# Seven block products for eight in the layers' down projection

## What is computed

```python
def conv_ffn(hn, w_up, conv_w, conv_b, w_down):
    u = depthwise_conv_centred(hn @ w_up, conv_w, conv_b)
    gate, val = jnp.split(u, 2, axis=-1)
    return (jax.nn.gelu(gate, approximate=True) * val) @ w_down

for l in range(DEPTH_2):                                   # 2 layers
    mixed = hybrid_mixer(rms_norm(x, mix_pre_g[l]), ...)
    x = x + rms_norm(mixed, mix_post_g[l])
    ff = conv_ffn(rms_norm(x, ffn_pre_g[l]), w_up[l], ...)
    x = x + rms_norm(ff, ffn_post_g[l])
```

## Time and profile before

| | us |
|---|---|
| median of 3 runs | 2075.01 (2074.34 to 2078.17) |
| the profiled execution | 2079.1 |
| its span, first to last instruction | 2077.4 |
| TensorE busy | 1974.8 (95%) |
| VectorE busy | 597.2 (29%) |
| ScalarE busy | 409.3 (20%) |
| GpSimd busy | 92.5 (4%) |

### The profile page before, as it was taken

How to read it: one execution, slowest core, us unless ns; L and a number is a source line. 1 busy time by engine, 2 the same in 40 slices (tenths; PEclk the granted TensorE clock), 3 DMA queues, 4 the chain that set the end, 5 groups by cost and what they waited for, 6 DMA issues and landing times.

```text
span 2077.4 us, 22981 instructions
## 1 busy us (share of the span) xinstructions
PE 1974.8 (95%) x9060; PEld 1137.3 (55%) x9060; DVE 597.2 (29%) x1240; ACT 409.3 (20%) x868; POOL 92.5 (4%) x167
## 2 busy tenths in 40 slices
PE   6999999999989899999898999999999999999998
PEld 2767885333333333333333334766888456778863
DVE  1387513122112112211121122542333035333311
ACT  2134213111111001111110112243222023422110
POOL 0000000000000000000000000200000011000000
PEclk9999999999999999999999999999999999999999
DMA  9655358999999999999999998153454334335430
GB/s 377 236 195 206 129 203 322 411 427 427 428 427 428 428 427 428 428 427 427 428 428 428 428 427 341 40 204 112 143 162 162 120 114 162 122 122 162 162 139 24
DMA packets 132852, 582.20 MB, mean 280 GB/s; under 512 B 9608, under 2 KB 55824, under 8 KB 106416
## 3 DMA queue, kind: packets, MB, share of 16 engines
q1 hardware_dynamic: 128240, 574.70, 69.5%
q0 software_dynamic: 4544, 6.57, 1.0%
HBM read 580.18 MB, written 2.63 MB: 281 GB/s over the span
## 4 chain that ended last, share of the span: by engine, by line
PE 74%; DMA 21%; DVE 3%; ACT 1%; issue 1%; SPq 0%; DVEq 0%; ACTq 0%
PE psum L357 52%; PE psum L675 11%; DMA work<-w_gu 11%; DMA ring<-w_gu 9%; PE psum L620 9%; PE psum L2118 1%; DVE work L1778 1%; PE psum L662 1%; DMA ring<-w_in 1%; PE psum L651 1%; DMA ring<-w_ada 0%; PE psum L1052 0%; ACT work L2439 0%; SPq L459 0%; DVE work L1776 0%
## 5 line engine op out<-in xcount | busy, mean ns | idle before, releaser
L357 PE MATMUL psum<-normed,ring 128*128 128x256 f32 (+1 forms) x2432 | 507.5, 370 | 0.2 <-PE psum L357 0.2
L357 PEld LDWEIGHTS psum<-normed,ring 128*128 128x128 f32 x2432 | 443.0, 191 | 60.8 <-issue 4.7
L620 PE MATMUL psum<-ring,normed 128*64 128x512 f32 x1024 | 234.5, 611 | 35.0 <-DMA ring<-w_gu 33.8
L620 PE MATMUL psum<-work,normed 128*64 128x512 f32 x1024 | 232.6, 608 | 33.1 <-DMA work<-w_gu 33.1
L357 PE MATMUL psum<-ring,work 128*128 128x512 f32 (+1 forms) x592 | 249.8, 581 | 0.1
L357 PE MATMUL psum<-work 128*128 128x128 f32 (+7 forms) x1152 | 185.1, 334 | 2.5 <-ACT work L2429 1.7
L357 PEld LDWEIGHTS psum<-ring,work 128*128 128x128 f32 x592 | 111.7, 190 | 130.6 <-issue 129.3
L620 PEld LDWEIGHTS psum<-ring,normed 128*64 128x64 f32 x1024 | 81.0, 141 | 186.3 <-issue 184.1
L620 PEld LDWEIGHTS psum<-work,normed 128*64 128x64 f32 x1024 | 80.5, 140 | 183.6 <-issue 183.6
L357 PEld LDWEIGHTS psum<-work 128*128 128x128 f32 (+2 forms) x1152 | 135.1, 186 | 65.0 <-issue 52.0
L357 PE MATMUL psum<-ring,normed 128*128 128x512 f32 (+2 forms) x400 | 160.5, 557 | 2.2 <-DMA ring<-w_in 1.8
(11 more groups left out here) (304 smaller groups left out, 1326.7 us busy)
## 6 DMA issues: line engine op xcount, KB each, us to landing
ring<-w_gu SPq DMA_DIRECT2D x64, 2048.0 KB, 27.4
work<-w_gu SPq DMA_DIRECT2D x64, 2048.0 KB, 27.5
work<-w_dn SPq DMA_DIRECT2D x32, 2048.0 KB, 27.4
ring<-w_dn SPq DMA_DIRECT2D x28, 2048.0 KB, 27.4
ring<-w_in SPq DMA_DIRECT2D x25, 2048.0 KB, 9.2
ring<-w_up SPq DMA_DIRECT2D x44, 1024.0 KB, 7.3
ring<-w_ada SPq DMA_DIRECT2D x11, 2048.0 KB, 9.4
ring<-w_down SPq DMA_DIRECT2D x10, 2048.0 KB, 7.8
```

The lines of the kernel that those rows point to most:

```text
L357: return pe.matmul(out, lhsT, rhs, start=first, stop=last, **kw)
L620: ins = pe.matmul(b[r], self.hgT[:, 2 * q + k, r], ws[e][:, k, n0:n0 + 512], start=q == 0 and k == 0, stop=q == QUARTERS - 1 and k == 1, s ...
```

## The change

Chunks 0 to 15 are taken as 8 pairs (SEVENS = 8), a pair a, b = 2i, 2i + 1. For a pair, the 2x2 blocks are A[t][k] = the tokens t of chunk k, and B[k][j] = half j of the weights of chunk k. Their product, four output blocks with two products each, is formed from seven products (Winograd's form of Strassen's algorithm) of these operands:

- tokens: A11, A12, A22 as they are, and four sums S1 = A21 + A22, S2 = S1 - A11, S3 = A11 - A21, S4 = A12 - S2. GpSimd makes them for four pairs at a time, 128x512 per operation, when eight chunks of `hid` are ready. They lie in SBUF where the attention's inputs were.
- weights: B11, B21 as they are, T1 = B12 - B11, T3 = B22 - B12 (written over B12 in the ring slot), T2 = B22 - T1, T4 = B21 - T2. VectorE makes them pair by pair, four operations of 128x512. T1, T2, T4 go into one of two buffers; the sums for pair i wait for TensorE to be through with pair i - 2 (`weight_sums_used`).

The seven products of all eight pairs add up in seven PSUM banks; three of these are directly output blocks (`down` (0,0), (0,1), (1,0)), four are named `sum`. After the eighth pair ScalarE copies `sum` 1 and VectorE combines the `sum` banks into four totals in SBUF (`sevens_totals`). Chunks 16 to 21 are done as before, four products each, on top of the three output banks and, for (1,1), in a bank of its own. VectorE then adds each finished bank to its total, and `post_norm` goes on from the total in SBUF.

The core of the diff:

```diff
-    u += [("down", l, t, j) for t in tiles for j in range(2)]
+    u += [("sum", l, 1), ("down", l, 0, 0), ("down", l, 0, 1), ("sum", l, 7), ("down", l, 1, 0), ("sum", l, 5), ("sum", l, 6), ("down", l, 1, 1)]
...
+            for g in range(SEVENS // 4):
+                pool.wait_ge(hid_ready, l * FC + 8 * g + 8)
+                pairs = hid[:, 8 * g:8 * g + 8].rearrange("p (i k) t -> p i k t", k=2)
+                a11, a12, a21, a22 = (pairs[:, :, k, t * P:(t + 1) * P] for t in range(2) for k in range(2))
+                s1, s2, s3, s4 = (s_sums[:, i, 4 * g:4 * g + 4] for i in range(4))
+                step(pool.tensor_tensor(s1, a21, a22, ALU.add))
+                step(pool.tensor_tensor(s3, a11, a21, ALU.subtract))
+                step(pool.tensor_tensor(s2, s1, a11, ALU.subtract))
+                pool.tensor_tensor(s4, a12, s2, ALU.subtract).then_inc(s_ready, 1)
...
-            for d in range(4):
-                w = weights(d)
-                for k in range(4):
-                    if (d, k) == (0, 0):
-                        pe.wait_ge(hid_ready, l * FC + 16)
-                    for t in range(NT):
-                        for j in range(2):
-                            ins = product(t, j, 4 * d + k, w[:, k])
-                ins.then_inc(down_used, 1)
+            def seven(i, w):
+                a, b = 2 * i, 2 * i + 1
+                wa, wb = w[:, a % 4], w[:, b % 4]
...
+                total(1, product(("sum", l, 1), tokens(a, 0), half(wa, 0), True))
+                product(("down", l, 0, 0), tokens(b, 0), half(wb, 0))
+                product(("down", l, 0, 1), s_sums[:, 3, i], half(wb, 1))
+                pe.wait_ge(t_ready, l * SEVENS + i + 1)
+                total(7, product(("sum", l, 7), s_sums[:, 2, i], half(wa, 1), True))
+                ins = product(("down", l, 1, 0), tokens(b, 1), t_sums[:, i % 2, 2])
+                if i % 2 == 1:
+                    ins.then_inc(down_used, 1)
+                total(5, product(("sum", l, 5), s_sums[:, 0, i], t_sums[:, i % 2, 0], True))
+                ins = product(("sum", l, 6), s_sums[:, 1, i], t_sums[:, i % 2, 1], True)
+                if last:
+                    total(6, ins)
+                else:
+                    ins.then_inc(t_used, 1)
...
             for t in range(NT):
                 for j in range(2):
-                    if (t, j) == (1, 1) and l + 1 < LAYERS:
-                        norm_transposes(l + 1, 0, 0)
-                    for k in range(16, FC):
-                        ins = product(t, j, k, ws[k // 4 - 4][:, k % 4])
+                    if (t, j) == (1, 1):
+                        empty("down", l, 1, 1)
+                    for k in range(2 * SEVENS, FC):
+                        if (t, j, k) == (1, 1, FC - 3) and l + 1 < LAYERS:
+                            norm_transposes(l + 1, 0, 0)
+                        ins = matmul(pe, bank("down", l, t, j), tokens(k, t), half(ws[k // 4 - SEVENS // 2][:, k % 4], j),
+                                     (t, j, k) == (1, 1, 2 * SEVENS), k == FC - 1)
                     ins.then_inc(*B.fills("down", l, t, j))
...
+            take(totals[:, 1], bank("sum", l, 1), "sum", l, 1)        # ScalarE
...
+                if s == 1:
+                    total = totals[:, 1 + 2 * t + j]
+                    filled("down", l, t, j)
+                    take(TT(total, bank("down", l, t, j), total, ALU.add), "down", l, t, j)
+                    step(TT(half(xn[:, t], j), total, half(post[:, s], j), ALU.mult))
+                    continue
...
+            def weight_sums(i):
+                if i >= 2:
+                    dve.wait_ge(t_used, l * (SEVENS - 1) + i - 1)
+                if i % 2 == 0:
+                    dve.wait_ge(*S.ready("down", l, i // 2))
+                w = slot(S.no(("down", l, i // 2)), 4, D)
+                wa, wb = w[:, 2 * i % 4], w[:, 2 * i % 4 + 1]
+                t1, t2, t4 = (t_sums[:, i % 2, n] for n in range(3))
+                step(TT(t1, half(wa, 1), half(wa, 0), ALU.subtract))
+                step(TT(half(wa, 1), half(wb, 1), half(wa, 1), ALU.subtract))
+                step(TT(t2, half(wb, 1), t1, ALU.subtract))
+                TT(t4, half(wb, 0), t2, ALU.subtract).then_inc(t_ready, 1)
+
+            def sevens_totals():
+                both, s00, s01, s10, s11 = (totals[:, n] for n in range(5))
+                dve.wait_ge(*B.released("sum", l, 1))
+                filled("sum", l, 6)
+                take(TT(both, bank("sum", l, 6), s00, ALU.add), "sum", l, 6)
+                step(TT(s01, bank("sum", l, 5), both, ALU.add))
+                filled("sum", l, 7)
+                take(TT(s10, bank("sum", l, 7), both, ALU.add), "sum", l, 7)
+                take(TT(s11, bank("sum", l, 5), s10, ALU.add), "sum", l, 5)
+
             for c in range(FC):
                 outer_taps(c)
                 if c >= 1:
                     hidden(c - 1)
+                if c in (FC - 2, FC - 1):
+                    weight_sums(c - (FC - 2))
             hidden(FC - 1)
+            for i in range(2, SEVENS):
+                weight_sums(i)
+            sevens_totals()
             post_norm(l, 1, 0)
```

More of the change, by code:

```diff
@@ L2005, in second_block @@
     taps = Arena(mem.work, ex_at).take(3, 2, L)
+    s_sums = Arena(mem.work, aqk_at).take(4, SEVENS, P)
+    t_sums = Arena(mem.work, mqk_at).take(2, 3, 512)
+    totals = Arena(mem.work, mqk_at).take(5, 512)
+    assert aqk_at + 4 * SEVENS * P <= hid_at and SEVENS % 4 == 0 and SEVENS * 2 == FC - FC % 4 - 4
     assert hid_at + FC * L <= mqk_at
@@ L2324, in down @@
         def down(l):
-            for t in range(NT):
-                for j in range(2):
-                    empty("down", l, t, j)
-            def product(t, j, k, w):
-                return matmul(pe, bank("down", l, t, j), hid[:, k, t * P:(t + 1) * P], w[:, j * 512:(j + 1) * 512], k == 0, k == FC - 1)
             def weights(d):
@@ L2334, in weights, with tokens @@
                 return slot(S.no(("down", l, d)), min(4, FC - 4 * d), D)
[L2336 to L2344 removed]
+            def tokens(k, t):
+                return hid[:, k, t * P:(t + 1) * P]
@@ new lines, in seven, with product, total @@
+            def seven(i, w):
+                a, b = 2 * i, 2 * i + 1
+                wa, wb = w[:, a % 4], w[:, b % 4]
+                last = i == SEVENS - 1
+                def product(name, lhsT, rhs, ends=False):
+                    if i == 0:
+                        empty(*name)
+                    return matmul(pe, bank(*name), lhsT, rhs, i == 0, ends and last)
+                def total(n, ins):
+                    if last:
+                        ins.then_inc(*B.fills("sum", l, n))
+                total(1, product(("sum", l, 1), tokens(a, 0), half(wa, 0), True))
[8 more added lines that the diff above has]
+                ins = product(("sum", l, 6), s_sums[:, 1, i], t_sums[:, i % 2, 1], True)
+                if last:
+                    total(6, ins)
+                else:
+                    ins.then_inc(t_used, 1)
@@ L2345, in down @@
+            pe.wait_ge(hid_ready, l * FC + 2 * SEVENS)
+            for i in range(SEVENS):
+                if i % 4 == 0:
+                    pe.wait_ge(s_ready, l * (SEVENS // 4) + i // 4 + 1)
+                if i % 2 == 0:
+                    w = weights(i // 2)
+                seven(i, w)
             pe.wait_ge(hid_ready, (l + 1) * FC)
-            ws = [weights(d) for d in range(4, DOWN_SLOTS)]
+            ws = [weights(d) for d in range(SEVENS // 2, DOWN_SLOTS)]
             for t in range(NT):
@@ L2454, in pre_norm @@
                 else:
[L2455 to L2456 removed]
+                    act.wait_ge(*(B.released("mix", l, t, j) if s == 1 else (x_new, 4 * (l - 1) + 2 * t + j + 1)))
                 squares(half(x[:, t], j), ssq, n, j)
@@ L2467, in post_norm @@
             for j in range(2):
-                act.wait_ge(*B.ready(kinds[s], l, t, j))
-                squares(bank(kinds[s], l, t, j), psq, n, j, post_squared)
+                act.wait_ge(*(B.released("down", l, t, j) if s == 1 else B.ready("mix", l, t, j)))
+                squares(totals[:, 1 + 2 * t + j] if s == 1 else bank("mix", l, t, j), psq, n, j, post_squared)
             mean_root(psq, pr, n).then_inc(post_rstd, 1)
@@ L2645, in post_norm @@
             for j in range(2):
-                take(STT(out=half(x[:, t], j), in0=half(xn[:, t], j), scalar=pr[:, n, 1:2], in1=half(x[:, t], j), op0=ALU.mult, op1=ALU.add),
-                     kinds[s], l, t, j)
+                ins = STT(out=half(x[:, t], j), in0=half(xn[:, t], j), scalar=pr[:, n, 1:2], in1=half(x[:, t], j), op0=ALU.mult, op1=ALU.add)
+                if s == 1:
+                    signal(ins, x_new, 4 * l + 2 * t + j + 1)
+                else:
+                    take(ins, "mix", l, t, j)
         def conv(l, p):
```

22 lines of the change are left out of this document (12 added, 10 removed).

## The result

The changed kernel takes 2062.11 us (median of 4 runs, 2061.07 to 2063.57) where the kernel before took 2074.70 us beside it (4 runs, 2074.34 to 2078.17): a ratio of 0.9935, 95% interval 0.9921 to 0.9949. The forecast was 2060.8 us, with a range of 2058.0 to 2065.0. The profiled run of the changed kernel took 2061.15 us (span 2059.4 us), that of the kernel before 2079.1 us (span 2077.4).

The account below looks back on a forecast made before the run. It took the down projections to be paced by TensorE's number of products. Terms of -13.73, +0.2, -0.98 and +0.26 sum to -14.25 us, from 2075.0 to 2060.8 us; range 2058.0 to 2065.0.

Parts of the forecast that it names:

- Term 1: Down projections: 80 products for 88 per layer at 0.858 us each, saving 6.87 us a layer, 13.73 us in two.
- Term 2: Down projections: some 15 more waits per layer on TensorE's products, taken as 0.1 us a layer, 0.2 us in all.
- Term 3: End of layer 0: longer chain but three more products of cover; idle goes, transposes take 0.87 for 1.09 us; gain 0.98 us.
- Term 4: End of layer 1: the chain longer by an addition is not covered by products, costing 0.26 us.
- waits that are not free: Rival, 12%: each met wait breaks TensorE's stream by up to 0.1 us; gain shrinks by up to 3 us, 2062 to 2064.
- The sums in time: Down projections: VectorE's weight sums, 0.692 us each, cost TensorE nothing; narrowest place is pair 1 with 1.8 us to spare.
- the rival's working: Rival, 3%: VectorE sets the down projections' pace from 1.50 us per operation; at 9.3 us a pair, 2111 us.
- What I feared for `up`: In `up`, each of four GpSimd operations may hold up VectorE's `hidden` by up to 1.4 us, at zero cost.
- late next: After layer 0's end, the new x^T must be in `normed` before layer 1's first product; holds by 1.3 us.
- the narrower one: Run time if the forecast as worked out holds: 2059.5 to 2062.0 us, given 75%.

Follow-up runs that it names:

- eight_products: Changed kernel with each pair's first product computed twice, so eight products a pair, all waits and sums kept: 2075.16 us, ratio 0.9997.
- no_weight_sums2: Changed kernel without all weight sums, their waits and counts; products take plain weight halves, slots are counted free a little later: 2063.25 us, ratio 0.9940.
- transposes_alone: Kernel before the change, with only the transposes of the next layer's x moved three products later: 2078.18 us in a single run.
- token_sums_late: Changed kernel with GpSimd's second group of token sums waiting for all 22 chunks of `hid`, beside the weight sums: 2060.11 us in a single run.
- the second measurement: The changed kernel timed again with no edit: 2061.92 us against 2075.87 us, ratio 0.9934.

## Why the prediction was right

Its steps against the traces (us, negative is faster):

| step | forecast | measured | from |
|---|---|---|---|
| Term 1, 16 products | -13.73 | -13.74 | 7.85 - 0.98 and 6.87; eight_products -6.87 and -6.86 |
| Term 2, waits | +0.20 | 0.00 | no_weight_sums2, 69.91 in both; 76.78 with eight_products, 76.81 in transposes_alone |
| Term 3, layer 0's end | -0.98 | -0.98 | 77.76 - 76.78 in eight_products; transposes_alone -0.95 |
| Term 4, layer 1's end | +0.26 | +0.26 | 1.96 for 1.70 us to the reciprocal |
| sum | -14.25 | -14.46 | trace: 785.58 - 771.11 = 14.47 |
| not in the sum: output at the end | 0 | about -0.14 | 4.02 for 4.16 us, from spans given to 0.1 us |

**What bounds it.** Right: TensorE paced the stage by its number of products and still does. Taking the eighth product back gives the old time (ratio 0.9997); leaving out VectorE's part changes nothing.

**The waits.** The one term with a doubtful size was too large. Its 0.1 us a layer was a choice between 0 and 0.6, not a reading. Waits that are met cost nothing visible, and the rival "waits that are not free" falls with it. The 0.04 us that a chunk of `up` takes beyond its products are not its waits, or not all of them; what they are stays open.

**The sums in time.** Right in size and place: 0.69 us each, 1.8 us to spare at pair 1. The point from which VectorE paces, 6.01 us for a pair, has one experiment on either side (5.8 us: only the start waits; 8.7 us: eight waits and 1.8% slower than before). What the rival's working left out is the clock: waits of 2 us and more can bring slow products behind them, 6.8 of 24.5 us in layer 0. By its own working 8.7 us a pair would lose 6 x 2.7 us at pairs 2 to 7 and about 4 us at pair 1, 20 us in all, which is 13 us more than the stage before. The run shows 16.7 us more (94.42 - 77.76), 24.5 more than the changed kernel's stage, so the 18 us for 9.3 us a pair was too low as well. The waits alone (17.8 us, with one of 3.06 us at pair 0 that the working did not have) came to less than its 20.

**GpSimd.** I took 1.4 us for an operation of 128x512; they took 1.26 each:

```profile
1513.56 1.26 POOL L2113 TENSOR_TENSOR work<-work 128x512 f32<-128x512 f32 x1 [65.98 <-DVE work L2878]
```

Nothing hung on it. What I feared for `up`, that GpSimd holds VectorE up there by up to 1.4 us an operation, did not happen in layer 0: both groups of token sums (1513.56 to 1518.86 and 1568.79 to 1574.10 us) start just behind a `hidden` and end before the next one, and the outer taps beside them, which read a bank of PSUM, keep their 0.48 us (at 1517.76 and 1573.01 us). The cost of zero was right, the hold-up ahead of it was not seen there. That two operations with both inputs in SBUF do hold each other up, and that even this costs the stage nothing at pairs 2 and 3, token_sums_late shows.

**The ends.** Term 3 holds with its parts: three more products of cover take 0.76 us of idle time and 0.22 us of slower transposes away. What I called late next, `normed`, was ready at 1667.46 us, 1.6 us before TensorE was through (1669.03), forecast 1.3.

**From the trace to the time.** 2062.11 us is in the range, and 0.1 us above the narrower one (2059.5 to 2062.0) that stood for the forecast as worked out; the second measurement, 2061.92, is inside. Which side of such a bound it falls on is luck. The forecast subtracts the sum from a median of three runs. The stage is known to some 0.05 us, but the time of a run to no better than the first block's wander of 6 us; that the median came out 1.3 us above the forecast and not 0.4 us below it lies within that.

## What to carry to other kernels

Where the profile shows one engine at 99% of a stage at full clock and the others nearly empty, the price of what you take from it can be read from two marks a known number of operations apart; here it held to 0.01 us in 6.87. The extra work elsewhere is free until a pair of deadlines closes: look for the start, where the first sums stand in a queue behind older work, and for the end, where the combination needs products to lie under; taking two more pairs saved 1.7 us a layer and cost 6.5 in layer 0 and 2.6 in layer 1. Compare stages between marks that both kernels have, not whole runs, when code ahead of the change wanders by more than the effect.

## What the runs showed of the hardware

- A wait of about 2 us on TensorE can cost more than itself. After 2.06 us idle (with 0.16 us shortly before) the granted clock was 0.72 over the next 6 us and three products took 4.25 us for 2.74; after 2.05 us (with 0.17) in the layer before it stayed at 1.00. After 4.51 us idle eight transposes took 1.97 us for 1.04, at a granted clock of 0.50, the lower level (1.2 GHz). A mean of 0.72 says that a part of the 6 us was spent at it. From these rows it can't be told in advance whether the clock falls.
- VectorE and GpSimd, each in a chain of operations with two inputs in SBUF, take turns: 1.64 us for 0.69 and 1.59 us for 1.26. Neither starves. An outer tap of VectorE that reads PSUM keeps its 0.48 us beside the same GpSimd operation.
- TensorE's eight met waits and seven counts among 80 products cost 0.00 us in 69.91.
- A float32 product of 128x128x512 takes 0.858 us whether an operand comes from the weights' ring or is a sum made by VectorE or GpSimd: 6.01 us for seven.
- Unchanged code of the first block ended up to 6.2 us apart in eleven traces, while the stretch from there to the last VectorE row, the same work in four of the kernels, was 771.09 to 771.12 us.
